# Up tiles ahead of the router: high and low tokens as one moving operand of 512 columns

## The chip, the cores and the metric

The kernel runs on one core of a Trainium2 chip. The metric is the device time of one execution in microseconds. Three runs of the kernel before took 2381.69 to 2386.47 us, the median is 2384.48.

## What is computed

The kernel computes a small model of four layers on 256 tokens of width 1024: attention in windows with a mixture of single-neuron experts behind it, a convolution with a second such mixture, and two more layers. The change touches the two expert mixtures alone:

```python
def peer_mixer(h, w_query, sub_keys, w_up, w_down):
    """Product-key retrieval over PEER_N_EXPERTS single-neuron experts."""
    ...
        q = (xc @ w_query).reshape(c, PEER_HEADS, 2, PEER_HALF_DIM).astype(jnp.float32)
        sc = jnp.einsum('chpd,hpnd->chpn', q, keys32)
        sv, si = lax.top_k(sc, PEER_TOPK)
    ...
        g = jax.nn.softmax(best, axis=-1)
        u = w_up[eidx]
        a = jnp.einsum('cd,chkd->chk', xc, u).astype(jnp.float32)
        act = (jax.nn.gelu(a, approximate=False) * g).astype(xc.dtype)
        vv = w_down[eidx]
        return jnp.einsum('chk,chkd->cd', act, vv)
```

There are 128 x 128 = 16384 experts, and each token picks 8 x 16 of them.

## The kernel before

Rather than gather the experts of each token, the kernel computes all 16384 for all 256 tokens and multiplies by a weight that is zero for those not picked. The experts of a layer form 128 tiles of 128. An up tile is a product of the tile's 128 experts (the weights of TensorE) with the 256 tokens (the moving operand) over 1024 channels, in 8 steps of 128. Its result stands in one half of a PSUM bank, 256 columns; GELU of it goes to `acts` in SBUF. After 128 up tiles come 128 down tiles, with moving operands of 512 columns.

Precision: every fp32 operand is split into a high part that TensorE takes exactly and a low part, the rest. A product is then high weights by high tokens, high weights by low tokens, low weights by high tokens. So an up tile has 8 x 3 = 24 matmuls of 256 columns each (line 999), all into the same half bank, and each with a weight load of its own.

Each unit of weights (one tile, 512 KB) passes four places. SyncE loads it into one of 4 buffers `raw` (line 690). ScalarE copies it to `wh`, rounded to the high part (`high`, line 1337), one of 2 buffers. VectorE writes raw minus high to `wl` (`low`, line 1727), also 2 buffers. TensorE uses both (`up`), first all products with high weights, then those with low ones. ScalarE may write the high part of tile t + 2 when TensorE has finished tile t (`units_used`), and SyncE may load anew when the low part is done (`lo_ready`).

The tiles alternate between banks 0 and 1; tile t waits until the GELU of tile t - 2 has read its bank (`gelu_done`). ScalarE's order is written out: GELU of tile t (line 1446), high part of tile t + 2, and so on (`tiles`). At tiles 26 and 54 it has the exponent of the softmax (`exponent`, line 1462) ahead of the high part and the GELU; exponent and GELU need different tables, each loaded when it is needed.

The first `FIRST` = 72 tiles of a layer run ahead of the router. Beside them VectorE finds the top 16 of each head (`top16`: MAX8, FIND_INDEX8, MATCH_REPLACE8, each with one input in SBUF), and then turns the places into keys (`pick`, lines 2058 to 2064: tensor-tensor operations over up to 2048 elements, with two inputs in SBUF). Between these steps stand the low parts, spread by an estimate of the time that each step takes (`between`, `LOW_EVERY` = 1250 ns). Ahead of tile 72 VectorE also builds the first one-hot matrices (`build`, lines 2079 and 2085). From tile 72 on the router's products run between the up tiles, with a GELU of its own (`late_gelu`), which also writes the buffer `late`; before tile 72 `late` isn't used.

GpSimd computes small row scales, issues a few DMAs (the last ahead of the up tiles loads `lanes`, line 760), and is idle through the up tiles.

Of the kernel before, what the change touches and what calls it, by code (L numbers as in the profile page):

```python
# [14 lines left out]
F32R = mybir.dt.float32r  # L15
# [3 lines left out]
ALU = mybir.AluOpType  # L19
ACT = mybir.ActivationFunctionType  # L20
AX = mybir.AxisListType.X

P = 128
# [225 lines left out]
def build(nc, d, out):  # L249
    ctx = ExitStack()  # L250
    with ctx:
# [5 lines left out]
        def sem(name):  # L257
            if name not in sems:
                sems[name] = ctx.enter_context(nc.semaphore(name))
            return sems[name]  # L260
# [11 lines left out]

        place_of = {}
        resid = place("resid", [P, TT, D])
        xh, xl = place("xh", [P, KT, SEQ], F32R), place("xl", [P, KT, SEQ], F32R)
        raw = place("raw", [P, RAW, UNIT])
        wh, wl = place("wh", [P, SPLIT, UNIT], F32R), place("wl", [P, SPLIT, UNIT], F32R)
        arena = place("arena", [P, ARENA])
# [226 lines left out]
        products, weighted = sem("router_products"), sem("experts_weighted")  # L505
        held, late_weighted = sem("router_weights_held"), sem("late_experts_weighted")
        gelu_done = sem("gelu_done")
        g_high, g_low = sem("gated_high"), sem("gated_low")
        y_ready = sem("gated_y_ready")
        roped = sem("roped")  # L510
# [12 lines left out]
        def unit_wait(base, i):  # L523

            return i * 4 + base
# [177 lines left out]
        def _(pool):  # L703
# [50 lines left out]
            for layer, done in enumerate(("wo", "conv")):  # L754
# [3 lines left out]
                    .then_inc(extra_loaded["keys"], 16)  # L758
                pool.wait_ge(x_low, XG[f"rescaled{layer}"] + 4)
                pool.dma_start(lanes[:], d["c_lanes"].partition_broadcast(P)).then_inc(extra_loaded["lanes"], 16)  # L760
                dump(done)
                if layer == 1:

# [33 lines left out]
        def _(pe):  # L797
# [163 lines left out]
            def peer(layer):  # L961
# [27 lines left out]
                def up(t, i=0):  # L989

                    n, b = u0 + t, t % 2
                    w = [x[:, n % SPLIT, :].rearrange("p (k e) -> p k e", k=KT) for x in (wh, wl)]
                    if t >= 2 or not isinstance(i, int):
                        pe.wait_ge(gelu_done, unit_wait(N_KEYS * layer + t - 1, i))
                    for part in range(2):
                        pe.wait_ge((hi_ready, lo_ready)[part], unit_wait(n + 1, i))
                        for k in range(KT):
                            for xp in range(2 - part):
                                last = pe.matmul(banks[b][:, 0:SEQ], lhsT=w[part][:, k, :], rhs=x_in[xp][:, k, :],  # L999
                                                 start=(k == 0 and part == 0 and xp == 0), stop=(k == KT - 1 and part == 1))  # L1000
                    last.then_inc(units_used, 1)
# [317 lines left out]
        def _(act):  # L1319
# [102 lines left out]
            def peer(layer):  # L1422
# [16 lines left out]
                u0, d0 = first_unit[f"up{layer}"], first_unit[f"down{layer}"]  # L1439
                assert issued[0] == u0 + SPLIT  # L1440

                def gelu(t, i=0):

                    act.wait_ge(units_used, unit_wait(u0 + t + 1, i))
                    dst = acts[:, bass.ds(i * 4 + t, 1), :].rearrange("p a b -> p (a b)")
                    act.activation(dst, banks[t % 2][:, 0:SEQ], ACT.Gelu).then_inc(gelu_done, 1)  # L1446

                def tiles(t0, t1):
                    first = t0 + (t1 - t0) % 4
                    for t in range(t0, first):  # L1450
                        gelu(t)
                        high(u0 + t + SPLIT)
                    with act.Fori(0, (t1 - first) // 4) as i:
                        for k in range(first, first + 4):
                            gelu(k, i)
                            high(u0 + k + SPLIT, i)

                def exponent(t):

# [5 lines left out]
                for t in range(TT):  # L1465
                    tiles(at, EXP_TILES[t])
                    exponent(t)
                    high(u0 + EXP_TILES[t] + SPLIT)
                    gelu(EXP_TILES[t])
                    at = EXP_TILES[t] + 1  # L1470
                tiles(at, FIRST)
                q0, late0 = QUADS * layer, (N_KEYS - FIRST - 1) * layer

# [1176 lines left out]
```

## Time and profile before

| | us |
|---|---|
| median of three runs | 2384.48 |
| the profiled execution | 2386.18 |
| its span, first to last instruction | 2384.3 |
| TensorE busy | 2337.2 |
| VectorE busy | 1688.2 |
| ScalarE busy | 1332.5 |
| GpSimd busy | 44.1 |

Busy times are the union of an engine's instructions; matmuls are pipelined, so a TensorE that is busy all the time is not one at its peak. The page of the profile names engines PE (TensorE's matmuls), PEld (its weight loads), DVE (VectorE), ACT (ScalarE), POOL (GpSimd) and SP (SyncE). L999 is line 999 of the kernel. The granted clock is 1.00 where TensorE runs at 2.4 GHz.

### The profile page before, as it was taken

The page shows a single profiled execution, that of the slowest core. Times are in us where ns is not written, and L with a number is a line of the kernel's source. Part 1 is how long each engine was busy: PE and PEld are TensorE (multiplying, and loading weights), DVE is VectorE, ACT ScalarE, POOL GpSimd, SP SyncE. Part 2 cuts the span into 40 slices and gives each one's busy share as a digit, 9 for nine tenths or more (in the row PEclk, how much of TensorE's full clock was granted, in tenths as well). Part 3 has the DMA queues.
Part 4 walks back from the last instruction along what each step waited for, and adds up shares of the span by engine and source line. Part 5 has one row for each costly group of instructions (what it writes and reads, how often), then busy time and mean ns, then how long its engine had stood idle before and what let it go on. Part 6 is the DMA issues. An engine that isn't in the chain of part 4 may idle for free.

```text
span 2384.3 us, 45063 instructions
## 1 busy us (share of the span) xinstructions
PE 2337.2 (98%) x15648; PEld 2096.6 (88%) x15648; DVE 1688.2 (71%) x3190; ACT 1332.5 (56%) x2506; POOL 44.1 (2%) x87
## 2 busy tenths in 40 slices
PE   8999999999999999999999999999999998899998
PEld 7889999999988888899999999988888887788776
DVE  5656996899755555675898799956556577667565
ACT  4545545777655555445455677755554455665554
POOL 1000000000000000000000000000000000000000
PEclk9999999999999999999999999999999999999999
DMA  7445666444566666565565544566666653246454
GB/s 234 124 141 156 177 187 179 143 142 142 169 193 194 194 194 192 161 185 187 168 179 182 160 143 142 157 196 192 202 195 178 183 175 100 71 125 197 129 159 141
DMA packets 137082, 397.44 MB, mean 167 GB/s; under 512 B 12321, under 2 KB 13521, under 8 KB 136177
## 3 DMA queue, kind: packets, MB, share of 16 engines
q1 hardware_dynamic: 134432, 384.97, 53.6%
q0 software_dynamic: 2512, 10.66, 1.3%
q8 instruction: 84, 1.38, 0.2%
q14 instruction: 54, 0.43, 0.1%
HBM read 394.54 MB, written 1.05 MB: 166 GB/s over the span
## 4 chain that ended last, share of the span: by engine, by line
PE 89%; DVE 5%; ACT 3%; issue 2%; DMA 0%; POOL 0%; DVEq 0%; ACTq 0%; POOLq 0%
PE bank L999 31%; PE bank L1015 29%; PE bank L897 12%; PE bank L903 7%; PE bank L1028 4%; PE bank L956 1%; PE bank L944 1%; ACT wh L1337 1%; DVE wl L1727 1%; PE bank L929 1%; PE bank L980 1%; DVE aux L1765 1%; PE bank L949 1%; PE bank L908 0%; ACT arena L1326 0%
## 5 line engine op out<-in xcount | busy, mean ns | idle before, releaser
L1727 DVE TENSOR_TENSOR wl<-raw,wh 128x1024 fp32r<-128x1024 f32 (+1 forms) x732 | 893.5, 1222 | 541.4 <-ACT wh L1337 530.0
L1337 ACT ACTIVATE wh<-raw 128x1024 fp32r<-128x1024 f32 (+1 forms) x732 | 771.7, 1055 | 639.8 <-PE bank L1015 337.3
L999 PE MATMUL bank<-xh,wh 128*128 128x256 f32 x2048 | 511.7, 288 | 0.0
L999 PE MATMUL bank<-xl,wh 128*128 128x256 f32 x2048 | 502.0, 283 | 0.0
L999 PEld LDWEIGHTS bank<-xl,wh 128*128 128x128 f32 x2048 | 392.9, 192 | 0.0
L999 PEld LDWEIGHTS bank<-xh,wh 128*128 128x128 f32 x2048 | 392.2, 192 | 0.5
L999 PE MATMUL bank<-xh,wl 128*128 128x256 f32 x2048 | 287.8, 283 | 0.0
L1015 PE MATMUL bank<-wh,gl 128*128 128x512 f32 x1008 | 270.1, 390 | 1.7 <-DVE gl L2109 1.7
L1015 PE MATMUL bank<-wh,gh 128*128 128x512 f32 x1008 | 269.8, 389 | 0.5 <-ACT gh L1510 0.5
L1015 PE MATMUL bank<-wl,gh 128*128 128x512 f32 x1008 | 269.4, 389 | 0.0
L999 PEld LDWEIGHTS bank<-xh,wl 128*128 128x128 f32 x2048 | 264.0, 192 | 0.9 <-DVE wl L1727 0.4
L1015 PEld LDWEIGHTS bank<-wh,gl 128*128 128x128 f32 x1008 | 188.8, 188 | 42.5 <-DVE gl L2109 3.5
L1015 PEld LDWEIGHTS bank<-wh,gh 128*128 128x128 f32 x1008 | 188.9, 188 | 40.0 <-ACT gh L1510 1.1
L1015 PEld LDWEIGHTS bank<-wl,gh 128*128 128x128 f32 x1008 | 189.2, 188 | 39.4
L1446 ACT ACTIVATE arena<-bank 128x256 f32 (+1 forms) x144 | 55.4, 384 | 212.1 <-PE bank L999 212.0
L1493 ACT ACTIVATE first<-onehot,weight_high 128x128 bf16<-128x128 bf16 x512 | 160.9, 399 | 0.0
L897 PE MATMUL bank<-wh,xh 128*128 128x512 f32 (+1 forms) x384 | 126.4, 411 | 1.0 <-ACT wh L1337 0.8
L897 PE MATMUL bank<-wh,xl 128*128 128x512 f32 (+1 forms) x384 | 119.5, 393 | 0.0
L2109 DVE TENSOR_TENSOR gl<-arena,gh 128x256 fp32r<-128x256 f32 x256 | 106.8, 417 | 0.0
L1028 PE MATMUL bank<-first,onehot 128*128 128x128 bf16 x1536 | 104.9, 220 | 0.6 <-ACT first L1493 0.6
L897 PE MATMUL bank<-wl,xh 128*128 128x512 f32 (+1 forms) x384 | 101.9, 387 | 1.1 <-DVE wl L1727 1.0
L1510 ACT ACTIVATE gh<-arena 128x256 fp32r (+1 forms) x256 | 102.2, 399 | 0.0
(295 smaller groups left out, 2695.8 us busy)
## 6 DMA issues: line engine op xcount, KB each, us to landing
raw<-in_w_upT SPq DMA_DIRECT2D x256, 512.0 KB, 3.6
raw<-in_w_down SPq DMA_DIRECT2D x256, 512.0 KB, 3.7
raw<-in_l_w_in SPq DMA_DIRECT2D x84, 512.0 KB, 3.6
raw<-in_peer_w_query SPq DMA_DIRECT2D x32, 512.0 KB, 4.2
raw<-in_l_w_out SPq DMA_DIRECT2D x28, 512.0 KB, 3.7
raw<-in_attn_w_qkv SPq DMA_DIRECT2D x24, 512.0 KB, 4.3
raw<-in_conv_w_in SPq DMA_DIRECT2D x24, 512.0 KB, 3.7
arena<-in_na_bias POOLq DMA_DIRECT2D x4, 1024.0 KB, 7.1
```

What stands on the lines that cost most here:

```text
L897: last = pe.matmul(bank(js[b])[:, 0:cols], lhsT=x[:, kt, b * P:(b + 1) * P], rhs=w[part][:, kk, :], **flags)
L903: last = pe.matmul(bank(js[b])[:, m * SEQ:(m + 1) * SEQ], lhsT=w[part][:, kk, c0:c0 + P], rhs=x[:, kt, :], **f)
L929: last = pe.matmul(bank(js[2 * c + b])[:, :], lhsT=lhs[xp][:, kt, b * P:(b + 1) * P], rhs=w[part][:, kk, :], start=kt == 0 and part == 0 a ...
L999: last = pe.matmul(banks[b][:, 0:SEQ], lhsT=w[part][:, k, :], rhs=x_in[xp][:, k, :], start=(k == 0 and part == 0 and xp == 0), stop=(k == ...
L1015: last = pe.matmul(banks[4 + 2 * m + h][:, :], lhsT=g[gp][:, m * P:(m + 1) * P], rhs=w[:, h * 512:(h + 1) * 512], start=start and part == ...
L1028: last = pe.matmul(banks[2 + q % OUTS][:, c * N_KEYS:(c + 1) * N_KEYS], lhsT=onehot[:, q % RING, c, 1, :], rhs=first[:, q % FIRSTS, p, c, ...
L1337: act.activation(wh[:, n % SPLIT, 0:kts * cols], raw[:, n % RAW, 0:kts * cols], ACT.Copy)\
L1446: act.activation(dst, banks[t % 2][:, 0:SEQ], ACT.Gelu).then_inc(gelu_done, 1)
L1493: ins = act.activation(first[:, q % FIRSTS, 0, c, :], onehot[:, q % RING, c, 0, :], ACT.Copy, scale=weight_high[:, c0:c0 + 1])
L1510: act.activation(gh[:, t % SPLIT, :], src, ACT.Copy).then_inc(g_high, 1)
L1727: tt(wl[:, n % SPLIT, 0:kts * cols], raw[:, n % RAW, 0:kts * cols], wh[:, n % SPLIT, 0:kts * cols].bitcast(F32), ALU.subtract).then_inc(lo ...
L2109: tt(gl[:, t % SPLIT, :], src, gh[:, t % SPLIT, :].bitcast(F32), ALU.subtract).then_inc(g_low, 1)
```

## The change

For the first 72 tiles of each layer the high and the low tokens become one moving operand: they now lie in one tensor `x_both`, and a matmul with high weights takes 2 x 256 = 512 columns, the high tokens' product into the left half of the bank and the low tokens' into the right half. The 8 matmuls with low weights stay, into the left half. ScalarE copies the whole bank to `late` (512 columns), GpSimd adds its two halves into `acts`, and ScalarE takes the GELU there, in place. The bank is free for TensorE when the copy is done (`up_copied`). ScalarE's order becomes: copy of tile t, high part of tile t + 2, GELU of tile t, which waits for GpSimd's sum (`up_summed`). Tiles from 72 on keep their 24 matmuls.

```diff
-        xh, xl = place("xh", [P, KT, SEQ], F32R), place("xl", [P, KT, SEQ], F32R)
+        x_both = place("x_both", [P, 2, KT, SEQ], F32R)
+        xh, xl = x_both[:, 0], x_both[:, 1]
...
+                with pool.Fori(0, FIRST // 4) as i:
+                    for t in range(4):
+                        pool.wait_ge(up_copied, unit_wait(FIRST * layer + t + 1, i))
+                        pool.tensor_tensor(acts[:, bass.ds(i * 4 + t, 1), :].rearrange("p a b -> p (a b)"), late[:, 0], late[:, 1], ALU.add)\
+                            .then_inc(up_summed, 1)
...
-                    if t >= 2 or not isinstance(i, int):
-                        pe.wait_ge(gelu_done, unit_wait(N_KEYS * layer + t - 1, i))
+                    if t >= FIRST + 2:
+                        pe.wait_ge(gelu_done, N_KEYS * layer + t - 1)
+                    elif t >= 2 or not isinstance(i, int):
+                        pe.wait_ge(up_copied, unit_wait(FIRST * layer + t - 1, i))
+                    if t < FIRST:
+                        pe.wait_ge(hi_ready, unit_wait(n + 1, i))
+                        for k in range(KT):
+                            pe.matmul(banks[b].rearrange("p (a b) -> p a b", a=2), lhsT=w[0][:, k, :], rhs=x_both[:, :, k, :],
+                                      start=k == 0, stop=False, skip_group_check=True)
+                        pe.wait_ge(lo_ready, unit_wait(n + 1, i))
+                        for k in range(KT):
+                            last = pe.matmul(banks[b][:, 0:SEQ], lhsT=w[1][:, k, :], rhs=xh[:, k, :], start=False, stop=k == KT - 1,
+                                             skip_group_check=True)
+                        last.then_inc(units_used, 1)
+                        return
...
+                def copy_halves(t, i=0):
+
+                    act.wait_ge(units_used, unit_wait(u0 + t + 1, i))
+                    act.activation(late[:].rearrange("p a b -> p (a b)"), banks[t % 2][:, :], ACT.Copy).then_inc(up_copied, 1)
+
                 def gelu(t, i=0):
 
-                    act.wait_ge(units_used, unit_wait(u0 + t + 1, i))
+                    act.wait_ge(up_summed, unit_wait(FIRST * layer + t + 1, i))
                     dst = acts[:, bass.ds(i * 4 + t, 1), :].rearrange("p a b -> p (a b)")
-                    act.activation(dst, banks[t % 2][:, 0:SEQ], ACT.Gelu).then_inc(gelu_done, 1)
+                    act.activation(dst, dst, ACT.Gelu).then_inc(gelu_done, 1)
 
                 def tiles(t0, t1):
                     first = t0 + (t1 - t0) % 4
                     for t in range(t0, first):
+                        copy_halves(t)
+                        high(u0 + t + SPLIT)
                         gelu(t)
-                        high(u0 + t + SPLIT)
                     with act.Fori(0, (t1 - first) // 4) as i:
                         for k in range(first, first + 4):
+                            copy_halves(k, i)
+                            high(u0 + k + SPLIT, i)
                             gelu(k, i)
-                            high(u0 + k + SPLIT, i)
...
                     exponent(t)
-                    high(u0 + EXP_TILES[t] + SPLIT)
-                    gelu(EXP_TILES[t])
-                    at = EXP_TILES[t] + 1
+                    at = EXP_TILES[t]
```

## Rows read from the trace of the kernel before

**Rows 1.** The page: TensorE's busy time, and the chain that ended last, by line.
```profile
PE 2337.2 (98%) x15648; PEld 2096.6 (88%) x15648; DVE 1688.2 (71%) x3190; ACT 1332.5 (56%) x2506; POOL 44.1 (2%) x87
PE bank L999 31%; PE bank L1015 29%; PE bank L897 12%; PE bank L903 7%; PE bank L1028 4%; PE bank L956 1%; PE bank L944 1%; ACT wh L1337 1%; DVE wl L1727 1%; PE bank L929 1%; PE bank L980 1%; DVE aux L1765 1%; PE bank L949 1%; PE bank L908 0%; ACT arena L1326 0%
```
**Rows 2.** Busy by stretch: window, its length, engines, clock, DMA share, GB/s.
```profile
209.90:421.00 211.10, 211.10 (x1753) 210.38 (x1752) 176.88 (x537) 104.42 (x155) 0.00 (x0) 1.00 0.60 175
580.00:900.00 320.00, 320.00 (x1679) 272.45 (x1677) 200.50 (x278) 171.48 (x307) 0.00 (x0) 1.00 0.62 185
1129.00:1342.00 213.00, 213.00 (x1772) 212.36 (x1771) 177.76 (x537) 105.09 (x158) 0.00 (x0) 1.00 0.58 174
```
**Rows 3.** Waits of VectorE, 216 to 419: us in total, times, longest.
```profile
DVE wl L1727 <- ACT wh L1337: 30.4, 48, 3.2
```
**Rows 4.** Timeline of TensorE, up tiles: start, us, instruction.
```profile
326.20 0.28 PE L999 MATMUL bank<-xh,wh 128*128 128x256 f32 x1
...
329.08 0.28 PE L999 MATMUL bank<-xh,wh 128*128 128x256 f32 x1
...
331.00 1.12 PE L999 MATMUL bank<-xh,wl 128*128 128x256 f32 x8
```
**Rows 5.** Timeline of TensorE in the down stage.
```profile
702.51 1.07 PE L1015 MATMUL bank<-wl,gh 128*128 128x512 f32 x4
...
705.23 1.07 PE L1015 MATMUL bank<-wl,gh 128*128 128x512 f32 x4
```
**Rows 6.** Timeline of ScalarE behind the tile that ends at 329.08.
```profile
329.38 0.38 ACT L1446 ACTIVATE arena<-bank 128x256 f32 x1 [1.55 <-PE bank L999]
329.67 1.05 ACT L1337 ACTIVATE wh<-raw 128x1024 fp32r<-128x1024 f32 x1
```
**Rows 7.** Groups by form, ScalarE: busy us, mean ns, idle before.
```profile
L1326 ACT ACTIVATE arena<-bank 128x512 f32<-128x512 f32 x43 | 25.5, 593 | 3.1 <-PE bank L1113 2.3
```
**Rows 8.** The page's groups: VectorE's 256-column subtraction.
```profile
L2109 DVE TENSOR_TENSOR gl<-arena,gh 128x256 fp32r<-128x256 f32 x256 | 106.8, 417 | 0.0
```
**Rows 9.** Timeline of VectorE, a low part among the maxima.
```profile
327.87 1.23 DVE L1727 TENSOR_TENSOR wl<-raw,wh 128x1024 fp32r<-128x1024 f32 x1 [0.22 <-ACT wh L1337]
```
**Rows 10.** Timelines of GpSimd and VectorE: a tiny add alone and beside VectorE.
```profile
19.68 0.19 POOL L718 TENSOR_TENSOR small<-small 128x2 f32<-128x2 f32 x1 [17.00 <-ACT aux L1376]
...
161.70 0.98 POOL L718 TENSOR_TENSOR small<-small 128x2 f32<-128x2 f32 x1 [89.14 <-ACT aux L1376]
...
161.40 2.43 DVE L1727 TENSOR_TENSOR wl<-raw,wh 128x1024 fp32r<-128x1024 f32 x2
```
**Rows 11.** Timelines of VectorE and TensorE around the picks.
```profile
275.25 1.22 DVE L1727 TENSOR_TENSOR wl<-raw,wh 128x1024 fp32r<-128x1024 f32 x1 [0.20 <-ACT wh L1337]
...
291.74 1.21 DVE L1727 TENSOR_TENSOR wl<-raw,wh 128x1024 fp32r<-128x1024 f32 x1
...
359.62 1.23 DVE L1727 TENSOR_TENSOR wl<-raw,wh 128x1024 fp32r<-128x1024 f32 x1 [0.45 <-ACT wh L1337]
...
373.26 1.23 DVE L1727 TENSOR_TENSOR wl<-raw,wh 128x1024 fp32r<-128x1024 f32 x1
...
284.07 1.12 PE L999 MATMUL bank<-xh,wl 128*128 128x256 f32 x8
...
293.24 1.00 PE L999 MATMUL bank<-xh,wl 128*128 128x256 f32 x7
...
368.44 1.12 PE L999 MATMUL bank<-xh,wl 128*128 128x256 f32 x8
...
374.56 1.20 PE L999 MATMUL bank<-xh,wl 128*128 128x256 f32 x8
```
**Rows 12.** Timelines of VectorE and TensorE at the builds.
```profile
416.07 1.22 DVE L1727 TENSOR_TENSOR wl<-raw,wh 128x1024 fp32r<-128x1024 f32 x1
...
418.15 1.12 PE L999 MATMUL bank<-xh,wl 128*128 128x256 f32 x8
```
**Rows 13.** Timeline of ScalarE: the exponent's table load.
```profile
286.68 1.28 ACT L1462 ACT_TABLE_LOAD   x1
```

More of the change, by code:

```diff
@@ L507, in build @@
         gelu_done = sem("gelu_done")
+        up_copied, up_summed = sem("up_halves_copied"), sem("up_halves_summed")
         g_high, g_low = sem("gated_high"), sem("gated_low")
```

## Prediction

> **What bounds the kernel now.** I read the page first: TensorE is busy 98% of the span, no other engine over 71%, and TensorE's line 999 alone, the up tiles, makes 31% of the chain that ended last [rows 1]. So whatever TensorE spends less in those tiles counts, as long as nothing else becomes late. Second view, the busy time by stretches: in the stretch of the 72 up tiles ahead of the router of either layer TensorE is busy without a gap, at a granted clock of 1.00 (2.4 GHz), and VectorE is the next fullest with 177 of 211 us; GpSimd does nothing [rows 2]. Third, the waits in that stretch: VectorE waits for ScalarE's high parts 48 times for 30.4 us in all [rows 3], and nothing is listed for TensorE. That sum hides two places, which only the timeline shows (below).
>
> Inside a tile TensorE starts a 256-column matmul every 0.120 us: one tile starts at 326.20, the next at 329.08, 2.88 us for 24 matmuls, and that one's matmuls with low weights at 331.00, behind 16 with high weights [rows 4]. In the down stage, 512-column matmuls, also each with its own weight load, start 0.2267 us apart: rows of four, and from the first row to the fourth 705.23 - 702.51 = 2.72 us for 12 starts [rows 5]. Twice 256 columns is 0.240 us, one times 512 is 0.2267.
>
> **The change part by part.**
>
> *Matmuls.* Per tile 16 matmuls of 256 columns become 8 of 512; the 8 with low weights stay. 8 x (0.240 - 0.2267) = 0.107 us per tile, so 2.77 us instead of 2.88; 72 tiles x 2 layers = 144 tiles give 15.4 us. This is all there is to win: columns streamed are the same, only the fixed part of a start goes. The moving operand becomes two pieces of 256 columns, 8 KB apart, which no row shows; I take it at the price of a plain one, bounds 0.2267 and 0.240.
>
> *ScalarE.* In steady state a tile ends at 329.08, its GELU starts at 329.38 and the high part at 329.67, 1.05 long [rows 6]. Now the first instruction is the copy of the whole bank; a 512-column copy out of PSUM takes 0.593 [rows 7]. GELU held ScalarE's queue for 0.29 of its 0.384, so the copy holds it for 0.50: the high part comes 0.21 later. The GELU in SBUF comes behind it and waits for GpSimd. ScalarE's work is 0.50 + 1.08 + 0.29 = 1.87 of 2.77 us, so it doesn't bind. The wait's round trip: copy starts 0.30 after the tile, ends at 0.90, the add takes X, GELU 0.38; the next copy is due at 2.77 + 0.30. With 0.1 for the signals X may be 1.6 before the next copy is late, and the high part has 0.9 us more of room before TensorE waits (it ends at 0.30 + 0.50 + 1.05 = 1.85 of 2.77). Queued behind the waiting GELU are just that copy and high part; VectorE's low part and TensorE wait for those in turn.
>
> *GpSimd.* 144 adds of 128x256. It has nothing else to do there; its DMA of the lanes is issued before the loop. Its price isn't in the trace. Nearest below: VectorE does this shape, SBUF to SBUF, in 0.417 [rows 8]; nearest above: VectorE's 1.22 for four times as many columns [rows 9]. GpSimd needs 0.19 for 2 columns where nothing disturbs it [rows 10]. For the add I take 0.6: the shape's own row, with a GpSimd that is slower per column; ends 0.4 and 1.2.
> The Trainium skill (GPSIMD Engine Reference, section 3) measures such an add at 2048 columns as 4497 ns, about twice VectorE; scaled it would be an estimate of 0.7 here. No run shown here has it.
>
> *What GpSimd and VectorE do to each other.* The same 2-column add of GpSimd, 0.19 long at 19.68, took 0.98 at 161.70 and ended at 162.68, just behind the first of the two 1.2 us subtractions that VectorE began at 161.40 [rows 10]. So GpSimd stood still until VectorE's instruction with two SBUF inputs was over. The other direction, VectorE standing still for a GpSimd operation of some length, isn't in the trace, since all of GpSimd's are tiny. I take it as symmetric: each add costs VectorE its 0.6 us where VectorE has two-input instructions queued, and nothing elsewhere.
> The Trainium skill (SBUF — State Buffer, Who interferes with whom) says that whichever issues first gets the shared port pair for its whole instruction and the other fully blocks, and that this holds for VectorE instructions with two SBUF inputs, not for those with one. The trace agrees for GpSimd's side, 0.98 against 0.19; this rule speaks against the change.
>
> *Where it hits.* In most tiles VectorE does one-input work (maxima, indices) and its low part starts when the high part ends, 1.87 after the tile's end; the add then lies at 0.95 to 1.55, so they miss each other. VectorE needs 2.66 us for such a tile (2.88 less the 0.22 that it waits [rows 9]), which fits in 2.77. The slack of a low part (its end to the matmul that uses it) is 331.00 - 329.10 = 1.90 us [rows 4, 9]. It falls by 0.21 (later high part), 0.107 (the shorter tile between) and 0.107 (the shorter high half): to 1.47.
> Two places per layer are different. From 275.25 to 291.74 VectorE has back-to-back two-input work (2048-element products over the picks), 16.49 us for five low parts, against 5 x 2.88 = 14.40 of TensorE; the slack is used up and TensorE loses 293.24 - 284.07 - 3 x 2.88 = 0.53 us. The second, from 359.62 to 373.26, is 13.64 us for four; the last of them ends at 374.49, its matmul starts at 374.56, and TensorE has lost 374.56 - 368.44 - 2 x 2.88 = 0.36 [rows 11]. The second layer's stretch is as full [rows 2]; I take it to repeat both.
> Without any contention the new kernel needs there: first place 16.49 - 5 x 2.77 = 2.64 over, less 1.42 of slack that can be used, = 1.2 lost instead of 0.5; second 13.64 - 4 x 2.77 = 2.56, less 1.42, = 1.1 instead of 0.4. So 0.75 more each, 4 x 0.75 = 3.0 us given back.
> With contention: five adds fall in the first place, 4.5 in the second (the tile behind it has no slack yet), 19 in both layers. 19 x 0.6 = 11.4 us. The bounds: 0 (VectorE never held), 19 x 0.42 = 8.0, 19 x 1.2 = 22.8.
> The expert builds ahead of tile 72 are such a burst too: the low part at 416.07 ends 0.86 ahead of its matmul at 418.15 [rows 12]. 0.86 - 0.43 - 0.6 is below zero by 0.2; with the shorter period, 0.3 per layer, 0.7 in all.
>
> *Small things.* The exponent's table load of 1.28 us [rows 13] and the one back to GELU stood ahead of a high part and of a GELU; now they stand ahead of a bank copy and of the next one, which come up to 1.3 late. This is inside the first place (and the second), where TensorE waits for VectorE anyway; I cost it at nothing as long as that cover lasts, up to 0.5 x 4 = 2 without it. In layer 0 the first GELU's table load no longer stands ahead of the third tile's high part: 0.1 gained. DMA moves 175 GB/s in the stretch [rows 2] and would need 524 KB / 2.77 = 189; the stretch 580 to 900 ran at 185 with TensorE fully busy [rows 2], so I cost it at nothing. From tile 72 on no instruction changes.
>
> *Sum.* -15.4 - 0.1 + 3.0 + 11.4 + 0.7 = -0.4 us. The profiled execution took 2386.18 (span 2384.3), 1.7 above the median 2384.48; taken off the median: 2384.1.
> By the page's 0.7 instead of 0.6 the sum would be 19 x 0.1 = 1.9 higher, +1.5.
>
> **The rivals.**
>
> *A, the main one:* the saving is eaten in the four places where VectorE binds. 2384, from -4.7 (a hold of 0.4 per add: 3.8 less) to +4.
>
> *B, VectorE is never held:* only GpSimd waits, as in the one direction that rows show. Then -15.4 - 0.1 + 3.0 + 0.2 = -12.3: 2372. For it: no row shows the other direction. Against it: a port that stops one side has to be given to the other at some time.
>
> *C, the add is long:* with the upper bound of 1.2 us it costs 22.8 in the four places and 1.5 at the builds, and it reaches to 2.15 after the tile's end, past the start of the low part at 1.87; that shifts VectorE once per tile by 0.3, which slack takes. -15.5 + 3.0 + 22.8 + 1.5 = +11.8: 2396. It decides for slower from a hold of about 0.85 (0.6 + 5/19).
>
> *D, the loop closes:* copy, add and GELU take longer than the tile, X over 1.6. With X at 2.0 each of 144 tiles is 0.4 longer: +58 - 15, some 2427. Against: only if GpSimd needs three times the 0.6.
>
> *E, the pair isn't cheaper:* at 0.240 per two-piece matmul nothing is saved, and the places cost 11.4 + 0.8 (later high part): +12, 2396.
>
> **How the numbers follow.** A 0.42, B 0.27, C 0.20, D 0.05, E 0.06. The likeliest gives 2384.1. About 0.2% (4.8 us) is what a measurement of this kernel can tell from no change. Faster: B, and the lower edge of A, 0.34. Slower: D and E, most of C, 0.27. Same: 0.39. The range goes from B's 2372 with 1 us off to where C is half in, 2371 to 2392; A's own is 2380 to 2388.
>
> **What would show it.** Matmuls with the two-piece operand: a pitch of 0.227, steady tiles of 2.77 apart. GpSimd's add: about 0.6 long in tiles with one-input work, longer where VectorE's products run. VectorE's products and low parts in the four places: records of more than 1.25 us, or gaps in front of them, 0.6 per tile; tiles there 3.6 apart instead of 3.0. If these records stay at 1.23 and follow without a gap, B holds. Waits of ScalarE for GpSimd of more than a few tenths in the steady tiles would point to C or D. The prediction is wrong if steady tiles are not at 2.77, or if the four places together lose far from 15 us.

## The result

The changed kernel takes 2390.95 us, the kernel before 2384.48 (medians of 13 runs each): the ratio is 1.0026, 95% interval 1.0018 to 1.0035. It is slower by a quarter of a per cent, 6.5 us, and the interval leaves no change out. The forecast was 2384.1, no change, with the range 2371 to 2392: the time lies inside the range, but it moved, and upward.

The profiled execution took 2390.95 (span 2389.1). The page of the profile after, busy times and the chain by line, against [rows 1]:

```profile
PE 2330.6 (98%) x14496; PEld 2033.8 (85%) x14496; DVE 1705.9 (71%) x3190; ACT 1453.3 (61%) x2676; POOL 163.7 (7%) x231
PE bank L1035 29%; PE bank L1019 13%; PE bank L904 12%; PE bank L1007 9%; PE bank L910 7%; PE bank L1011 5%; PE bank L1048 4%; DVE wl L1752 2%; PE bank L963 1%; PE bank L951 1%; ACT wh L1357 1%; PE bank L936 1%; PE bank L987 1%; PE bank L956 1%; DVE pick L2086 0%
```

TensorE is busy 6.6 us less, on 1152 fewer matmuls, and in the chain VectorE's low parts (line 1752) have 2% instead of 1%, with a trace of its products (line 2086). The changed kernel's stretches between up and down tiles, columns as in [rows 2]:

```profile
209.90:421.00 211.10, 206.10 (x1167) 177.74 (x1166) 183.24 (x533) 163.02 (x236) 58.87 (x71) 1.00 0.56 172
1129.00:1342.00 213.00, 207.88 (x1192) 180.02 (x1192) 181.05 (x530) 164.64 (x239) 57.71 (x70) 1.00 0.57 173
```

Its waits in the first of the two stretches (who waited for whom: us in all, times, us at most):

```profile
DVE wl L1752 <- ACT wh L1357: 23.2, 28, 2.0
PEld bank L1011 <- DVE wl L1752: 9.6, 11, 1.6
ACT arena L1471 <- POOL arena L766: 6.9, 13, 1.1
PE bank L1011 <- DVE wl L1752: 4.8, 6, 1.2
```

And from its page, the group of the adds:

```profile
L766 POOL TENSOR_TENSOR arena<-late 128x256 f32 x144 | 119.6, 831 | 335.7 <-ACT late L1465 335.7
```

TensorE had no gap there before (one of its weight loads waited 0.2 us for VectorE, which the prediction passed over); now it is idle 5.0 us of the first stretch, and all but a little of that is a wait for VectorE's low part. ScalarE has 59 us more work there.

The length that the experiments are compared by is one layer's stretch from the first up tile's matmul to the first down tile's; the granted clock is 1.00 all through it, so it isn't touched by what the clock does elsewhere. Before it is 417.2 and 416.9 us in the two layers, after 419.1 and 419.4: 4.4 us longer in all. Each length is that of one profiled execution, and all of them can be read to about 0.1 us. The spans of the two profiled executions differ by 4.8 us, so their difference is nearly all in the stretches; the medians differ by 6.5. The other 2 us lie outside the stretches. Runs of the changed kernel come at a mean granted clock of 0.994 (2387.9 to 2391.0 us) or 0.992 (2392.2 to 2394.4), those of the kernel before, as measured beside the experiments, at 0.993 to 0.995, and the profile of the changed kernel has one stretch at a granted clock of 0.50 (1.2 GHz) that the profile before doesn't have, from 983 on, 3.4 us long. Whether the change has a part in that stays open.

### The profile page after: what moved, and what is told of

It reads as the page before. It is cut to its first block, busy times and chain, and to the rows that moved or that the text cites. A ratio compares the mean times of both kernels' runs of the same rounds, so it can differ in the third digit from the quotient of the medians.

```text
span 2389.1 us, 43593 instructions
## 1 busy us (share of the span) xinstructions
PE 2330.6 (98%) x14496; PEld 2033.8 (85%) x14496; DVE 1705.9 (71%) x3190; ACT 1453.3 (61%) x2676; POOL 163.7 (7%) x231
## 4 chain that ended last, share of the span: by engine, by line
PE 86%; DVE 8%; ACT 3%; issue 2%; POOL 0%; DMA 0%; DVEq 0%; ACTq 0%; POOLq 0%
PE bank L1035 29%; PE bank L1019 13%; PE bank L904 12%; PE bank L1007 9%; PE bank L910 7%; PE bank L1011 5%; PE bank L1048 4%; DVE wl L1752 2%; PE bank L963 1%; PE bank L951 1%; ACT wh L1357 1%; PE bank L936 1%; PE bank L987 1%; PE bank L956 1%; DVE pick L2086 0%
## 5 line engine op out<-in xcount | busy, mean ns | idle before, releaser
L1007 PE MATMUL bank<-x_both,wh 128*128 128x512 f32 x1152 | 290.0, 394 | 0.0
L1019 PE MATMUL bank<-x_both,wh 128*128 128x256 f32 x1792 | 241.6, 288 | 0.0
L1007 PEld LDWEIGHTS bank<-x_both,wh 128*128 128x128 f32 x1152 | 206.9, 189 | 38.1 <-ACT wh L1357 0.3
L1019 PEld LDWEIGHTS bank<-x_both,wh 128*128 128x128 f32 x1792 | 221.6, 191 | 0.0
L904 PE MATMUL bank<-wh,x_both 128*128 128x512 f32 (+1 forms) x768 | 198.7, 401 | 1.0 <-ACT wh L1357 0.8
L1011 PEld LDWEIGHTS bank<-x_both,wl 128*128 128x128 f32 x1152 | 155.4, 190 | 28.9 <-DVE wl L1752 19.3
L1011 PE MATMUL bank<-x_both,wl 128*128 128x256 f32 x1152 | 162.9, 284 | 10.1 <-DVE wl L1752 9.6
L904 PEld LDWEIGHTS bank<-wh,x_both 128*128 128x128 f32 x768 | 141.0, 191 | 32.7 <-issue 5.6
L766 POOL TENSOR_TENSOR arena<-late 128x256 f32 x144 | 119.6, 831 | 335.7 <-ACT late L1465 335.7
L1465 ACT ACTIVATE late<-bank 128x512 f32<-128x512 f32 x144 | 85.7, 595 | 70.9 <-PE bank L1011 70.7
L1019 PE MATMUL bank<-x_both,wl 128*128 128x256 f32 x896 | 125.3, 283 | 0.0
L1019 PEld LDWEIGHTS bank<-x_both,wl 128*128 128x128 f32 x896 | 115.6, 192 | 0.0
```

The lines of the kernel that those rows point to most:

```text
L766: pool.tensor_tensor(acts[:, bass.ds(i * 4 + t, 1), :].rearrange("p a b -> p (a b)"), late[:, 0], late[:, 1], ALU.add)\
L904: last = pe.matmul(bank(js[b])[:, 0:cols], lhsT=x[:, kt, b * P:(b + 1) * P], rhs=w[part][:, kk, :], **flags)
L1007: pe.matmul(banks[b].rearrange("p (a b) -> p a b", a=2), lhsT=w[0][:, k, :], rhs=x_both[:, :, k, :], start=k == 0, stop=False, skip_group_ ...
L1011: last = pe.matmul(banks[b][:, 0:SEQ], lhsT=w[1][:, k, :], rhs=xh[:, k, :], start=False, stop=k == KT - 1, skip_group_check=True)
```

## Where the time went

TensorE's rows with low weights, one per tile; the distance of two is a tile. Changed kernel, steady (with the row of the eight 512-column matmuls between them), and then the first place around the picks:

```profile
331.33 1.12 PE L1011 MATMUL bank<-x_both,wl 128*128 128x256 f32 x8
332.29 2.00 PE L1007 MATMUL bank<-x_both,wh 128*128 128x512 f32 x8
334.13 1.11 PE L1011 MATMUL bank<-x_both,wl 128*128 128x256 f32 x8
...
276.51 1.11 PE L1011 MATMUL bank<-x_both,wl 128*128 128x256 f32 x8
279.57 1.22 PE L1011 MATMUL bank<-x_both,wl 128*128 128x256 f32 x8
283.64 1.22 PE L1011 MATMUL bank<-x_both,wl 128*128 128x256 f32 x8 [1.01 <-DVE wl L1752]
287.79 1.22 PE L1011 MATMUL bank<-x_both,wl 128*128 128x256 f32 x8 [1.09 <-DVE wl L1752]
290.92 1.22 PE L1011 MATMUL bank<-x_both,wl 128*128 128x256 f32 x8
294.24 1.22 PE L1011 MATMUL bank<-x_both,wl 128*128 128x256 f32 x8 [0.26 <-DVE wl L1752]
297.13 1.11 PE L1011 MATMUL bank<-x_both,wl 128*128 128x256 f32 x8
```

A steady tile takes 2.793 us (331.33 to 334.13 rounds it to 2.80), before 2.88 [rows 4]. The seven rows from 276.51 to 297.13 are six tiles apart: 20.62 us, where 6 x 2.793 = 16.76 would do. 3.9 us are lost, before 0.5 [rows 11]. The second place, seven tiles from 359.53 to 382.99, takes 23.46 us where 19.55 would do, and loses 3.9 too (before 0.4). The second layer repeats both within 0.1 us. The timelines of VectorE and GpSimd in the first place show why:

```profile
278.29 1.23 DVE L1752 TENSOR_TENSOR wl<-raw,wh 128x1024 fp32r<-128x1024 f32 x1
279.43 1.75 DVE L2086 TENSOR_TENSOR pick<-pick,key_of 128x2048 bf16<-128x2048 bf16 x1
...
281.94 1.64 DVE L1752 TENSOR_TENSOR wl<-raw,wh 128x1024 fp32r<-128x1024 f32 x1
...
286.09 1.65 DVE L1752 TENSOR_TENSOR wl<-raw,wh 128x1024 fp32r<-128x1024 f32 x1
287.66 1.21 DVE L2086 TENSOR_TENSOR pick<-pick,key_of 128x2048 bf16<-128x2048 bf16 x1
...
278.43 1.67 POOL L766 TENSOR_TENSOR arena<-late 128x256 f32 x1 [2.05 <-ACT late L1465]
281.61 0.90 POOL L766 TENSOR_TENSOR arena<-late 128x256 f32 x1 [1.51 <-ACT late L1465]
285.67 0.98 POOL L766 TENSOR_TENSOR arena<-late 128x256 f32 x1 [3.17 <-ACT late L1465]
```

The add recorded from 278.43, just behind the start of the low part at 278.29, waited for its end (279.5), then ran, and the product that VectorE began at 279.43 took 1.75 instead of 1.22: 0.53 of standing still. The low parts at 281.94 and 286.09 took 0.4 more for the adds begun at 281.61 and 285.67. So both directions are there. I call such a lengthening a hold. In the second place an add comes first and isn't disturbed itself, so the two directions don't mix:

```profile
362.47 0.74 POOL L766 TENSOR_TENSOR arena<-late 128x256 f32 x1 [2.49 <-ACT late L1465]
...
362.49 1.80 DVE L2083 TENSOR_TENSOR pick<-places,lanes 128x2048 bf16<-128x2048 bf16 x1
```

The add keeps its 0.74, and the product beside it takes 1.80 instead of 1.22: 0.58. The maxima and indices of the same stretch, with one input each, have the lengths of before (MAX8 0.43 to 0.49 a pair, FIND_INDEX8 0.27 to 0.29), though some 30 of the layer's 72 adds run beside nothing else of VectorE's.

## Experiments

All stretches are first up tile to first down tile, per layer, in us, first and second layer; the third column is the sum over both layers. In the expected texts theory H is that the holds cost the time, theory S that ScalarE's new order does.

| kernel | stretch | against 417.2, 416.9 | ratio of times, 95% interval |
|---|---|---|---|
| changed | 419.1, 419.4 | +4.4 | 1.0026 (1.0018 to 1.0035) |
| e1 tiny add | 419.8, 419.5 | +5.2 | 1.0024 (1.0014 to 1.0034) |
| e2 idle add on before | 421.7, 421.5 | +9.1 | 1.0048 (1.0035 to 1.0061) |
| e3 operand in one piece | 419.3, 419.4 | +4.6 | 1.0025 (1.0015 to 1.0035) |
| e4 four tiles out of the loop | 418.7, 418.7 | +3.3 | 1.0022 (1.0013 to 1.0030) |
| e6 tiny add, two buffers, e4 | 412.5, 412.7 | -8.9 | 0.9964 (0.9950 to 0.9977) |
| e7 hybrid | 413.5, 413.5 | -7.1 | 0.9974 (0.9964 to 0.9985) |
| e8 picks spread, e4 | 415.6, 415.5 | -3.0 | 0.9993 (0.9984 to 1.0002) |
| e9 picks spread on before | 416.9, 416.8 | -0.4 | 1.0002 (0.9993 to 1.0011) |
| e10 hybrid, two more tiles | 412.8, 412.9 | -8.4 | 0.9968 (0.9956 to 0.9980) |
| e11 half idle add on before | 419.0, 419.1 | +4.0 | 1.0027 (1.0017 to 1.0036) |
| e12 hybrid, fewer tiles | 413.4, 413.4 | -7.3 | 0.9977 (0.9968 to 0.9986) |

### e2 and e11: the add alone

```diff
+                pool.tensor_tensor(idle[:, :], xh[:, 0, :].bitcast(F32), xh[:, 1, :].bitcast(F32), ALU.add).then_inc(sem("idle_added"), 1)
+                with pool.Fori(0, FIRST // 4) as i:
+                    for t in range(4):
+                        pool.wait_ge(sem("idle_added"), unit_wait((FIRST + 1) * layer + t + 1, i))
+                        pool.wait_ge(gelu_done, unit_wait(N_KEYS * layer + t + 1, i))
+                        pool.tensor_tensor(idle[:, :], xh[:, 0, :].bitcast(F32), xh[:, 1, :].bitcast(F32), ALU.add).then_inc(sem("idle_added"), 1)
...
+                act.wait_ge(sem("idle_added"), (FIRST + 1) * (layer + 1))
```

> The kernel before, with one thing added: for each of the first 72 tiles of a layer GpSimd adds two 256-column pieces of the high tokens into a scratch, started by the tile's GELU; nobody waits for it inside the stretch. Nothing of the matmuls or of ScalarE's order changes. Theory H: each of the four places loses about 2.6 us more (five adds by 0.5), 10 to 11 us slower than before, and only there do TensorE's tiles get longer; VectorE's products of 1.23 appear as 1.6 to 1.8. Theory S: no change, within 1 us.

It came to 9.1 us in the stretches and 11.6 in the medians, against 10 to 11 expected. VectorE and GpSimd in the first place, e2:

```profile
281.01 1.76 DVE L2069 TENSOR_TENSOR pick<-pick,key_of 128x2048 bf16<-128x2048 bf16 x1
283.53 1.65 DVE L1735 TENSOR_TENSOR wl<-raw,wh 128x1024 fp32r<-128x1024 f32 x1
...
280.39 1.30 POOL L767 TENSOR_TENSOR idle<-xh 128x256 f32<-128x256 f32 x1 [2.10 <-ACT arena L1453]
283.27 0.83 POOL L767 TENSOR_TENSOR idle<-xh 128x256 f32<-128x256 f32 x1 [1.58 <-ACT arena L1453]
```

The same lengthened records as in the changed kernel, with ScalarE and TensorE as before. An add for which nobody waits costs 9.1 us, nearly three quarters of what the cheaper matmuls save (12.5, below), because of what it does to VectorE. e11 has the same diff with `[:, 0:128]`:

> The kernel before with the idle add of GpSimd at half its size, 128 columns instead of 256. With 256 columns the stretch from the first up tile to the first down tile grew from 417.1 to 421.6 us per layer, and a product of VectorE that met an add was 0.4 to 0.55 longer. If VectorE is held for as long as GpSimd reads (time by columns), the records are 0.2 to 0.3 longer and the stretch is about 419.3; if each add costs a fixed hold whatever its size, it stays near 421.6; GpSimd's own records go from 0.74 to about 0.47.

```profile
280.76 1.49 DVE L2069 TENSOR_TENSOR pick<-pick,key_of 128x2048 bf16<-128x2048 bf16 x1
287.03 1.37 DVE L1735 TENSOR_TENSOR wl<-raw,wh 128x1024 fp32r<-128x1024 f32 x1
```

And its group of adds from 215 to 415, nearly the whole part of the first stretch that has adds:

```profile
L767 POOL TENSOR_TENSOR idle<-xh 128x128 f32<-128x128 f32 x69 | 37.2, 539 | 181.0 <-ACT arena L1453 181.0
```

Half the columns: 1.49 and 1.37 for 1.76 and 1.65, so a hold of 0.14 to 0.28 where the changed kernel has 0.41 to 0.58, and a stretch of 419.05, near the middle, 419.3, between 417.05 and 421.6. The hold goes with the size of the add. An undisturbed add takes 0.74 at 256 columns and 0.46 at 128, so 0.28 for 128 columns, and the longest holds differ by 0.30: what grows with the columns is held, and some 0.2 us of each add are not. That the held part is the time of the reads fits this, but isn't shown.

### e1 and e6: the change with hardly an add

```diff
-                        pool.tensor_tensor(acts[:, bass.ds(i * 4 + t, 1), :].rearrange("p a b -> p (a b)"), late[:, 0], late[:, 1], ALU.add)\
+                        pool.tensor_tensor(idle[:, 0:2], late[:, 0, 0:2], late[:, 1, 0:2], ALU.add)\
...
+                    if t or layer:
+                        act.wait_ge(gelu_done, unit_wait(N_KEYS * layer + t, i))
...
-                    act.activation(dst, dst, ACT.Gelu).then_inc(gelu_done, 1)
+                    act.activation(dst, late[:, 0], ACT.Gelu).then_inc(gelu_done, 1)
```

> The changed kernel, but GpSimd adds only 2 of the 256 columns and the GELU reads the copied high-token products (the products of the low tokens are left out of the activations). All signals and ScalarE's order stay; one more wait of ScalarE for its own last GELU. Theory H (VectorE is held during GpSimd's reads): the four places around the picks lose 1.2 us each as worked out for no contention, not 3.9, so some 10.7 us less than the changed kernel: about 4 to 5 us faster than the kernel before, and VectorE's products and low parts there are back at 1.23. Theory S (ScalarE's later high parts, its round trip over GpSimd and its table loads cost the time): still 5 to 7 us slower than before, since ScalarE does the same.

It came out slower than before by 0.24%, 5.1 us, as the rival said, not faster: the expectation by theory H was missed. VectorE's products were back at 1.22, but the loss had moved. ScalarE of e1 in the middle of its loop, and TensorE's tiles there:

```profile
296.61 1.28 ACT L1468 ACT_TABLE_LOAD   x1 [1.01 <-PE bank L1012]
297.90 0.60 ACT L1468 ACTIVATE late<-bank 128x512 f32<-128x512 f32 x1
298.39 1.05 ACT L1358 ACTIVATE wh<-raw 128x1024 fp32r<-128x1024 f32 x1
299.46 1.28 ACT L1474 ACT_TABLE_LOAD   x1
300.75 0.42 ACT L1474 ACTIVATE arena<-late 128x256 f32 x1
...
298.18 1.11 PE L1012 MATMUL bank<-x_both,wl 128*128 128x256 f32 x8
301.47 1.10 PE L1012 MATMUL bank<-x_both,wl 128*128 128x256 f32 x8
304.80 1.12 PE L1012 MATMUL bank<-x_both,wl 128*128 128x256 f32 x8
```

Two table loads stand in one tile of every four, 2.57 us of ScalarE, and the wait for its own GELU, which I had added to keep one buffer safe, came on top: tiles of 3.3 us twice in four. The experiment had two changes at once. It doesn't refute the hold; it shows that ScalarE has no room for such a pair and another wait. e6 takes both away (against e1, the main lines):

```diff
+        lates = [late, place("late_b", [P, 2, SEQ], F32, at)]
...
-                    first = t0 + (t1 - t0) % 4
+                    first = t0 + ((t1 - t0) % 4 or 4)
```

> The tiny add once more (GpSimd adds 2 of 256 columns, the low tokens' products are left out of the activations), without what disturbed the first such kernel: tiles 26 to 29 of ScalarE are written out, so that no table loads stand in its loop, and the copies alternate between two buffers, so that ScalarE doesn't wait for its own GELU. Theory H: the steady tiles save 72 x 0.087 = 6.3 us per layer, the two places together lose 2.3 instead of 1.0, the router's head 0.6: 4.4 us per layer, 8.8 us faster than before. Theory S (ScalarE's order alone eats the saving): within 2 us of the time before or slower.

9.2 us faster in the median, 8.9 in the stretches, against 8.8 expected. TensorE and VectorE of e6 in the first place:

```profile
281.45 1.12 PE L1013 MATMUL bank<-x_both,wl 128*128 128x256 f32 x8
284.90 1.21 PE L1013 MATMUL bank<-x_both,wl 128*128 128x256 f32 x8 [0.49 <-DVE wl L1756]
288.02 1.22 PE L1013 MATMUL bank<-x_both,wl 128*128 128x256 f32 x8
290.92 1.18 PE L1013 MATMUL bank<-x_both,wl 128*128 128x256 f32 x8
...
277.89 1.22 DVE L2090 TENSOR_TENSOR pick<-pick,key_of 128x2048 bf16<-128x2048 bf16 x1
```

The two places together lose 2.3 us instead of the 7.8 of the changed kernel, as worked out for no contention. This is rival B's kernel: B's sum was 12.3 us faster, and the difference from 8.9 is mostly the saving that B's sum had 2.9 us too large. It leaves out part of the result, so it is no version to keep.

### e4: the table loads

```diff
-                    first = t0 + (t1 - t0) % 4
+                    first = t0 + ((t1 - t0) % 4 or 4)
```

> The changed kernel with tiles 26 to 29 of ScalarE's list written out ahead of its loop. In the changed kernel the trace has a table load at a copy and one at a GELU in every fourth tile from 30 to 53, six pairs per layer, where the kernel before has none. If the loop's unknown table at its head puts them there, they go, and with them the 0.12 us that TensorE loses after each: 1.2 to 1.6 us less than the changed kernel. If the pairs stay, they come from the change of instruction itself, and the time stays.

The pairs are gone and the stretches are 1.1 us shorter in all, a little under what was expected; the ratio alone (1.0022 against 1.0026) couldn't tell it. In the changed kernel the timeline of ScalarE has such a pair in every fourth tile of the second loop:

```profile
323.26 1.28 ACT L1465 ACT_TABLE_LOAD   x1
326.19 1.28 ACT L1471 ACT_TABLE_LOAD   x1
334.56 1.28 ACT L1465 ACT_TABLE_LOAD   x1
```

The loop is entered behind the exponent with one table and comes round with GELU's. That the first copy in its body is given a load for this reason, and the first GELU another, is read from where the loads stand; what e4 shows is that they go when the first turn is written out. The kernel before had one tile between exponent and loop.

Tile by tile the loads cost about twice the 1.1 us. (The time of a tile is taken here from the row with low weights of the one before to its own.) In the changed kernel tile 33 of each layer is 0.23 longer than a steady one, tiles 41, 45 and 49 are 0.13 to 0.16 longer each, and tile 53, at the head of the second place, is 0.5 longer. In e4 all this is gone but for a few hundredths, 2.3 us in both layers. But tile 28 takes 3.94 and 3.97 there instead of 3.32: in its place the low part at 292.68 takes 1.69, beside an add at 292.55, where the changed kernel's took 1.21. So what the loads had cost came back, more than half of it, as another hold.

### e3: one piece or two

```diff
-        x_both = place("x_both", [P, 2, KT, SEQ], F32R)
-        xh, xl = x_both[:, 0], x_both[:, 1]
+        x_both = place("x_both", [P, KT, 2, SEQ], F32R)
+        xh, xl = x_both[:, :, 0], x_both[:, :, 1]
```

> The changed kernel with the high and low tokens of a channel step side by side, so that the moving operand is one piece of 512 columns. In the changed kernel a steady tile takes 2.793 us, not 2.773: 8 matmuls at 0.229 rather than 0.2267. Theory P (the second piece costs it): the tile goes to 2.773, 144 x 0.02 = 2.9 us less than the changed kernel, about 3 to 4 us slower than before. Theory Q (the switch between 512 and 256 columns costs it, or the wait at the first matmul): the tile stays at 2.793 and the time too.

The tile stays at 2.793. The second piece costs nothing. Where the 0.02 us per tile go can be read from the starts of the single matmuls. The eight with 512 columns take 334.13 - 332.29 = 1.84 us, 0.230 each, and the eight with 256 columns 332.29 - 331.33 = 0.96. Of the eight the first five start 0.228 to 0.236 apart and the last three 0.227, in the changed kernel and in e3 alike; the first start among the 256-column ones comes 0.007 early. So the price of the down stage is reached only from the sixth on, behind a group of 256-column matmuls; why the first five are dearer stays open.

### e8 and e9: spreading VectorE's work

```diff
-EXP_TILES, SUM_TILES, CHOICE_TILES = (26, 54), (30, 59), (34, 62)
+EXP_TILES, SUM_TILES, CHOICE_TILES = (26, 54), (33, 62), (38, 66)
...
-                                 lane.to_broadcast([P, HK, TOPK // 2, 2]), ALU.is_equal), 1200)
+                                 lane.to_broadcast([P, HK, TOPK // 2, 2]), ALU.is_equal), 1250)
...
-                        pstep(tt(by_head, by_head, key_of[:, :, i].unsqueeze(2).to_broadcast([P, PEER_HEADS, TOPK, TOPK]), ALU.mult), 1200)
+                        pstep(tt(by_head, by_head, key_of[:, :, i].unsqueeze(2).to_broadcast([P, PEER_HEADS, TOPK, TOPK]), ALU.mult), 1250)
```

The last number of a step is the estimate of its time; at 1250 ns, `LOW_EVERY`, a low part follows it.

> The changed kernel with tiles 26 to 29 of ScalarE written out (no table loads in its loop) and VectorE's work around the picks spread: a low part stands behind each of the 2048-element products, so that at most some 1.7 us of work lie between two low parts instead of 2.5, and the picks end three to four tiles later (sums at tiles 33 and 62, turned choices at 38 and 66). Theory H in its simple form (work and holds sum up on VectorE, slack is what is missing): the places lose 1.5 to 2.5 us each instead of 3.9, so 6 to 9 us less than the changed kernel: 0 to 4 us faster than before. If order doesn't matter, only the 1.5 us of the table loads is gained: 4 to 5 us slower than before.

> The kernel before with the same spread of VectorE's work around the picks and nothing else. It loses 0.5 us in each of the four places; a low part behind each 2048-element product should take that away: 1.5 to 2 us faster than before, TensorE without a gap there. It is the fair base for the spread version of the change.

e8 came to 3.0 us below the kernel before in the stretches, which is inside what was expected; its time can't be told from that of the kernel before (0.9984 to 1.0002). Its places lose 2.9 and 1.9 us per layer, the first more than the 2.5 expected at most. e9 was a miss: 0.4 instead of 1.5 to 2. Its places lose 0.7 instead of 1.0 per layer, and its time can't be told from that of the kernel before (0.9993 to 1.0011). So the spread gains on the changed kernel, where the holds make the places long, and hardly on the one before.

### e7, e10, e12: the change only where it pays

```diff
+PLAIN = tuple(range(22, 30)) + tuple(range(50, 60))                # e7
+PLAIN = tuple(range(22, 30)) + tuple(range(50, 60)) + (70, 71)     # e10
+PLAIN = tuple(range(23, 29)) + tuple(range(51, 58)) + (70, 71)     # e12
```

(The labels behind `#` are mine.) In tiles of `PLAIN` all four engines do what the kernel before does; counts of copies and sums skip them. The full result is computed.

> The change applied only where VectorE has one-input work: tiles 22 to 29 and 50 to 59 keep their 24 matmuls, bank halves and GELU from the bank as before; the other 54 of 72 have the 512-column operand, copy and add. The full result is computed. Theory H: 54 x 0.087 = 4.7 us saved per layer, the places lose 1.0 as before, the router's head 0.6 and the builds 0.2 more: 3.9 us per layer, some 8 us faster than before. Theory S: the copy and GELU round trip costs in any tile, so the loss of the changed kernel shrinks only in proportion, to about 3 to 5 us slower than before.

> The hybrid with tiles 70 and 71 left as before too (52 of 72 changed). In the hybrid the router's first products come 0.6 us later, because ScalarE has the last tile's copy, its wait for GpSimd and its GELU ahead of the router's first weighting, and the builds' tile loses 0.2. If that is so, both go and 2 x 0.087 is given up: the stretch from the first up tile to the first down tile goes from 413.5 to about 412.9 per layer, 1.2 us less in all, some 8 us faster than before. If the router's head has another cause, 413.7.

> The same with fewer tiles left out: 23 to 28, 51 to 57, 70 and 71 keep their 24 matmuls, 57 of 72 are changed. If adds hold VectorE only while it has the picks' two-input products, the five more changed tiles save 0.44 us per layer: 412.5. If one more add falls into either place, it costs 0.5 each instead: 413.5 or more.

e7 came to 7.1 us faster in the stretches and 6.6 in the medians, against 8 expected. e10 came to 412.85 where 412.9 was expected, so the router's head is confirmed: from tile 72 to tile 73, with the router's first products between them, it is 4.75 us in the kernel before, 5.41 and 5.43 in the changed one, 5.34 in e7 and 4.65 in e10. ScalarE there in the changed kernel:

```profile
421.01 0.60 ACT L1465 ACTIVATE late<-bank 128x512 f32<-128x512 f32 x1 [0.18 <-PE bank L1011]
421.51 1.05 ACT L1357 ACTIVATE wh<-raw 128x1024 fp32r<-128x1024 f32 x1
422.70 0.42 ACT L1471 ACTIVATE arena<-arena  x1
423.02 2.14 ACT L1518 ACTIVATE first<-onehot,weight_high 128x128 bf16<-128x128 bf16 x7
```

And in e10, the same group of the router's instructions:

```profile
416.81 2.44 ACT L1567 ACTIVATE first<-onehot,weight_high 128x128 bf16<-128x128 bf16 x8
```

In the changed kernel copy, high part and GELU of tile 71 take from 421.01 to 423.02 before the router's first weights; in e10 tile 71's GELU, straight from PSUM, began at 415.58, and the weights follow 1.2 us behind it instead of 2.0 behind the copy. e12 came out as its second case: with five more tiles changed it is 413.4 rather than 412.5, since in each place one more add meets VectorE. In the first layer the operation at 275.12 takes 0.76 (0.29 in e10) and the cast at 355.82 takes 0.93 (0.49 in e10). e10 is the best version with the full result: 2376.64 us, ratio 0.9968 (0.9956 to 0.9980), 8.4 us faster than the kernel before in the same set of runs, and 14 than the changed one in another set.

## Why the prediction was right and wrong

*The saving: the step that failed.* The term "8 x (0.240 - 0.2267) = 0.107 us per tile", 15.4 us in all, took the price of a 512-column matmul from a stage where all matmuls have 512 columns [rows 5]. Measured: a tile of 2.793 us instead of 2.773, so 144 x 0.087 = 12.5 us. The eight matmuls cost 0.230 each rather than 0.2267: the first five behind the 256-column ones are dearer. The prediction gave bounds for this price, 0.2267 and 0.240, and then took the lower one in its sum. Its reason for doubt was the operand in two pieces, and e3 shows that this isn't it. This is the largest of its errors, 2.9 us.

*Small things: two terms put at nothing.* "The exponent's table load ... I cost it at nothing" looked only at the loads that were already there. That the loop would get a pair of its own in every fourth tile isn't in it; behind these pairs TensorE loses 1.3 us in both layers in tiles 33 to 49, and 1.0 more in tile 53, which is counted with the places below. I had read which engine waits at which tile, but not which table the loop is entered with. And "from tile 72 on no instruction changes" is so, but the first of them stand on ScalarE behind the last tile's copy and GELU. That costs 0.66 and 0.67 us, 1.3 in both layers. The builds, at 0.7 in the sum, cost 0.6.

*The four places: the mechanism right, the number in part by luck.* The forecast was that they lose 1.2 and 1.1 us per layer for lack of slack and 5.7 for the holds, 8.0 in all; the trace has 3.9 and 3.9. The lack of slack came out as worked out, 2.3 us per layer in e6. The holds are 0.41 to 0.58 instead of the 0.6 taken, and half a microsecond per layer is the table loads at tile 53, so the holds alone cost about 5.0, not 5.7. That VectorE is held at all was taken as symmetric from rows of one direction [rows 10]. e2 shows it alone, e11 that it goes with the size, e6 that without it the change is faster by what the rest of the sum says.
The Trainium skill (SBUF — State Buffer, Who interferes with whom) states this lock for both directions: for VectorE instructions with two SBUF inputs against a GpSimd instruction that reads SBUF, and also for instructions with one input in a mode that uses both ports, casts among them, which the prediction left out. The traces agree: 1.80 for a product of 1.22, and for a cast see the last section. That the lock lasts for the whole instruction is stated there for the two-port modes; here VectorE is held for 0.58 at most of an add of 0.74.
The Trainium skill (GPSIMD Engine Reference, section 3) has 4497 ns for 2048 columns. The prediction's estimate from it was 0.7, and the add measured 0.74; by columns alone it would be 0.56, so the agreement rests on a fixed part that the prediction didn't write down.

*The sum.* Tile by tile against the kernel before, both layers: -12.5 for the steady tiles, -0.1 for the third tile of layer 0, +13.8 for the places (7.8 and 7.9, where the kernel before loses 0.95 per layer), +1.3 for the table loads outside them, +0.6 for the builds, +1.3 for the router's head, +0.1 at the tiles where the choices are turned: +4.5, and the stretches say +4.4. The forecast's -0.4 differs from this by 2.9 + 1.3 + 1.3, less 0.6 for the places. The mechanism was right: the saving and the places nearly cancel. But the result is their small difference, and the errors in the saving, the loads and the router's head all have one sign. No single one of them gives the 6.5 us of the medians, and the 2 us by which the medians differ more than the stretches remain open.

*The rivals.* B is out: the lengthened records of the changed kernel, e2 and e6 show it from both sides. C: the hold is shorter than 0.6, not longer. D: ScalarE waited for GpSimd 6.9 us in the first stretch, most of it in the places and some at the builds, and in steady tiles hardly at all; but e1 shows how near it is, one wait and one pair of loads more were enough. E: a small part; of the 0.0133 us that a pair of 256-column matmuls costs more than one of 512, 0.0025 net were not saved.

## What to carry to other kernels

Before giving GpSimd an elementwise operation, look at what VectorE does at that moment, not at GpSimd's own share: where VectorE is the next bound and works on two SBUF inputs, each add costs it some 0.5 us here, and there it costs the kernel as much. A change that pays in most tiles and costs in a few can be left out of those few; here this turned +0.26% into -0.32%, and it took a look at each place: five tiles more (e12) gave back 1.1 us of it. With a saving of 0.1 us per tile, terms of 1 us (a table load that a loop's head brings in, the first instruction behind the loop) decide the sign, so list each engine's state at each loop's entry and exit.

## What the runs showed of the hardware

GpSimd's add of 128x256 takes 0.74 us from SBUF to SBUF where nothing disturbs it, and 0.46 at 128x128 (e11; 0.54 with the disturbed ones in the mean). VectorE instructions with two SBUF inputs that meet it are longer by 0.41 to 0.58 and by 0.14 to 0.28. Not only those: in the changed kernel the cast at 273.13 from 32-bit integers to fp32, with one input, took 0.92, and 0.49 before; I hadn't expected that. In e11 casts from fp32 to bf16 (128x256) took 0.44 instead of 0.29. Maxima and indices never got longer. VectorE's timeline of the changed kernel:

```profile
273.13 0.92 DVE L2070 CAST arena<-arena 128x640 f32<-128x640 uint32 x1
```

The same cast in the kernel before:

```profile
274.56 0.49 DVE L2045 CAST arena<-arena 128x640 f32<-128x640 uint32 x1
```

Matmuls of 512 columns start 0.2267 us apart among themselves, and 0.228 to 0.236 in the first five behind eight of 256 columns. A moving operand in two pieces 8 KB apart goes at the rate of one in one piece (2.793 us per tile both ways). A copy out of PSUM of 512 columns and a copy of 1024 within SBUF run under GELU's table without a load (e4); in the changed kernel two loads of 1.28 us stand in every turn of a loop that is entered behind the exponent, and writing out one turn ahead of it takes them away.
